# Differential attention whose scores contract all 128 rows against keys that are zero in the other component's rows

## The chip, the cores and the metric

The kernel runs on one core of one Trainium2 chip. The metric is the device time of one execution in microseconds (us); lower is better. Three executions of the kernel before took 3723.07, 3725.74 and 3731.34 us.

## The reference, cut to what matters

The model is a stack of five blocks on 512 tokens of width 1024: a first hybrid block, and then four layers with an mLSTM, a sliding-window attention, an HGRN2 and a differential attention as mixers, each followed by a feed-forward part. The change touches only the last mixer, the differential attention, with 8 heads of two components of 64 dimensions each:

```python
def diff_mixer(h, positions, lam_init, w_in, lam_vec, norm_w, w_out):
    ...
    q = partial_rope(proj[..., :w].reshape(bsz, seq, 2 * D_HEADS, D_HEAD_DIM), positions)
    k = partial_rope(proj[..., w:2 * w].reshape(bsz, seq, 2 * D_HEADS, D_HEAD_DIM), positions)
    ...
        s = jnp.einsum('bqhcd,bkhcd->bhcqk', qi, k, preferred_element_type=F32) * scale
        s = jnp.where(kpos[None, :] <= qpos[:, None], s, -jnp.inf)
        p = jax.nn.softmax(s, axis=-1)
        a = p[:, :, 0] - lam * p[:, :, 1]
        return jnp.einsum('bhqk,bkhe->bqhe', a, v)
```

Each component c of a head has its own 64 dimensions of queries and keys and its own softmax; the two weight matrices are subtracted and meet the same 128-wide values. Everything is float32.

## The kernel before, in words

Every engine runs a program written out by hand; they meet only through semaphores. `proj` holds the projections with features on the 128 partitions and tokens along the free dimension. In the differential layer, called part 3, tiles 0 to 7 of `proj` are the queries of heads 0 to 7 and tiles 8 to 15 are the keys. A head's component 0 lies in partitions 0 to 63 of its tile, and component 1 in partitions 64 to 127. The values lie in `df_v`.

The weights come as a stream of slots of 128x1024. For each slot SyncE issues a DMA, ScalarE makes the high part (line 1134), GpSimd subtracts it for the low part (`low`, line 532), and TensorE multiplies three times. The ring has four slots, so GpSimd is at most four slots ahead of TensorE: when the last value slot has been used, the last low part that can be made before the attention is that of the fourth slot of the output projection. The next needs a slot that the output projection frees, which comes after the attention.

VectorE copies the projected tiles out of PSUM and rotates them (`rope`, lines 1776 to 1778: a product with PSUM, a product of two SBUF tensors in place, and a sum of two SBUF tensors). In part 3 the query tiles are rotated before the first group of value tiles is copied out and the key tiles before the second. Then come the copies of the last values (line 1557), `lambdas` (lines 1941 to 1946, with one exponential on ScalarE), and one small copy (line 2040) that raises `mix_ready`, for which TensorE waits before its first score.

The attention is a pipeline over 64 jobs (`diff_jobs`): for each of 8 heads, for each of the 4 query blocks i of 128 tokens, for components 0 and 1. A job's score has (i+1)*128 keys. In step s TensorE issues the score of job s (line 802), the transposes of the weights of job s-2 (line 810, i+1 of them, full 128x128) and the products with the values of job s-3 (line 822, 128x128 each). VectorE adds the mask and takes the minimum (line 1626, from PSUM), and then scales the weights of the job before (line 1638 for component 0, line 1640 for component 1, from SBUF to SBUF). ScalarE makes the exponential (line 1224) and copies the transposed weights out of PSUM (line 1231). Before, a score is a matmul over the 64 rows of its component:

```python
jobs.append(job(proj[HD * c:HD * c + HD, hd, i * P:(i + 1) * P],
                proj[HD * c:HD * c + HD, 8 + hd, 0:w], w, lc[:, 768 - w:768],
```

A float32 matmul shows as two instructions in the trace, a transpose as one. The sliding-window layer and the dilated attention of the first block use the same `attention` function with full 128-row scores already, but with values of 64 columns. The stick-breaking code and the gated convolution of the first block (lines 580 to 587, on GpSimd) appear below only for their durations.

Of the kernel before, what the change touches and what calls it, by code (L numbers as in the profile page):

```python
# [8 lines left out]
F32 = mybir.dt.float32  # L9
# [3 lines left out]
ALU = mybir.AluOpType  # L13
# [3 lines left out]
P = 128  # L17
S = 512
D = 1024
DT = D // P  # L20
HD = 64
# [4 lines left out]
RING = 4  # L26
LEAD = 4
# [142 lines left out]
@contextmanager  # L170
def loop(eng, count):
    if count > 1:
        with eng.Fori(0, count) as i:
            yield i
    else:
        yield 0
# [16 lines left out]
def program(nc, xT, wstream, ada, cols, kept, bigc, layerc, pos, yT, parts):  # L193
    slots_total = stream_length(parts)
    ctx = ExitStack()
    with ctx:
# [82 lines left out]
        hg_p = [place(f"hg_p{r}", [P, TT, 640], F32, big + (16 + 4 * r) * S) for r in range(2)]  # L279
        hg_gate_at = [hg_k[:, 0, :]] + [proj[:, 8 + g, :] for g in range(7)]  # L280
        df_v = place("df_v", [P, TT, D], F32, big + 16 * S)

        bank = [ctx.enter_context(nc.psum_tensor(f"bank{b}", [P, S], F32)) for b in range(8)]

# [11 lines left out]
        def col(name, j=0, n=1):  # L296
# [29 lines left out]
                 "rope_ang", "ml_gate", "ml_pre", "ml_log", "ml_rows", "ml_turn", "ml_w", "ml_floor",  # L326
                 "ml_floor_kept", "ml_spread", "ml_diag", "ml_exp", "ml_a", "ml_den", "ml_num", "ml_out", "ml_sig",
                 "hg_lb", "hg_lbe", "hg_sig", "hg_dec", "hg_log", "hg_diff", "hg_e", "hg_qk", "hg_mm", "hg_put",
                 "hg_pv", "hg_out", "hg_gate", "hg_zero", "gate_kept", "lam_in", "lam_exp", "stored", "act_chain", "dve_chain"]
        sm = namedtuple("Semaphores", names)(*[ctx.enter_context(nc.semaphore(name)) for name in names])  # L330
        raw_loaded = [ctx.enter_context(nc.semaphore(f"raw_loaded{r}")) for r in range(RING)]
        ada_loaded = [ctx.enter_context(nc.semaphore(f"ada_loaded{r}")) for r in range(ADA_RING)]
# [4 lines left out]

        def job(q, k, width, bias_ap, values, **more):
            return dict(q=q, k=k, w=width, bias=bias_ap, v=values, sink=None, vis=None, gate=None, first=True,
                        last=True, dv=HD, row=0, dest=None) | more  # L340

        def head_pairs(heads):

# [44 lines left out]
        def diff_jobs():  # L388
            jobs = []
            for hd in range(8):  # L390
                for i in range(TT):
                    w = (i + 1) * P
                    for c in range(2):
                        jobs.append(job(proj[HD * c:HD * c + HD, hd, i * P:(i + 1) * P],
                                        proj[HD * c:HD * c + HD, 8 + hd, 0:w], w, lc[:, 768 - w:768],
                                        [(df_v[:, j, hd * P:(hd + 1) * P], P) for j in range(i + 1)],
                                        gate=lam if c else None, first=c == 0, last=c == 1, dv=P,
                                        dest=proj[:, hd, i * P:(i + 1) * P]))
            return jobs


# [126 lines left out]
        @block.gpsimd  # L528
        def _(pool):
            def low(k, i=0, step=0):  # L530
                pool.wait_ge(sm.hi_done, k + 1 + step * i)
                nc.gpsimd.tensor_tensor(w_lo[k % RING][:, :, :], raw[k % RING][:, :, :],  # L532
                                        w_hi[k % RING][:, :, :].bitcast(F32), ALU.subtract).then_inc(sm.lo_done, 1)

            def low_to(end):

                k, count = n["slot"], end - n["slot"]
                with loop(pool, count // RING) as i:
                    for q in range(RING):
                        low(k + q, i, RING)  # L540
                for q in range(count // RING * RING, count):
                    low(k + q)
                n.add(slot=count)

            def hgrn():

                for r in range(3):
                    nc.gpsimd.memset(hg_q[r][:, :], 0.0)
                    op = nc.gpsimd.memset(hg_t[r][:, :], 0.0)
                op.then_inc(sm.hg_zero, 1)  # L550
                pool.wait_ge(sm.hg_zero, 1)
                for hd in range(8):
                    for at in range(9):
                        m, i, b = hd * 10 + at, hd * 9 + at, LV[at]
                        if at == 6 and hd:
                            low(n["slot"])
                            n.add(slot=1)
                        pool.wait_ge(sm.hg_e, i + 1)
                        wait(pool, sm.hg_mm, m - 2)
                        d = halves(hg_d[i % 3][:, :], b)  # L560
                        nc.gpsimd.tensor_tensor(halves(hg_q[m % 3][:, :], b)[1], halves(proj[:, hd, :], b)[1], d[1],
                                                ALU.mult)
                        nc.gpsimd.tensor_tensor(halves(hg_t[m % 3][:, :], b)[0], halves(hg_k[:, hd, :], b)[0], d[0],
                                                ALU.mult).then_inc(sm.hg_qk, 2 if at == 8 else 1)

            n = Counts()
            def gated_convolution():

                g = nc.gpsimd
                steps = 0  # L570

                def link(ins):

                    nonlocal steps
                    steps += 1
                    ins.then_inc(sm.conv_step, 1)
                    pool.wait_ge(sm.conv_step, steps)

                pool.wait_ge(sm.lin_free, len(IN_PROJ["first"][0]))
                for t in range(2):  # L580
                    u, y, w = proj[:, 13 + t, :], proj[:, 11 + t, :], [col("conv_w", 3 * t + i) for i in range(3)]
                    link(g.tensor_tensor(u, u, y, ALU.mult))
                    link(g.tensor_scalar(y, u, w[2], None, ALU.mult))
                    for lag in (1, 2):
                        link(g.tensor_scalar(conv_tmp[:, lag:S], u[:, 0:S - lag], w[2 - lag], None, ALU.mult))
                        link(g.tensor_tensor(y[:, lag:S], y[:, lag:S], conv_tmp[:, lag:S], ALU.add))
                    link(g.tensor_tensor(proj[:, 2 + t, :], y, proj[:, 2 + t, :], ALU.mult))

            first_slot = 0
            for at, part in enumerate(parts):  # L590
                tiles, values = IN_PROJ[part]
                if part == "first":
                    low_to(len(tiles) + len(values) + 8 + LEAD)
                    gated_convolution()
                if part in (1, 3):
                    low_to(first_slot + LEAD)
                    pool.wait_ge(sm.lin_free, lin_total(parts[:at]))
                    pool.dma_start(rope_i[:, :], pos).then_inc(sm.pos_loaded, 16)
                if part == 2:
                    low_to(first_slot + len(tiles) + len(values) + LEAD)  # L600
                    hgrn()
                first_slot += stream_length([part])
            low_to(slots_total)
# [3 lines left out]
        def _(pe):  # L607
# [188 lines left out]
            def attention(jobs, bufs):  # L796
                a, g = n["att"], n["att_g"]
                for step in range(len(jobs) + 3):
                    if step < len(jobs):
                        j, it = step, jobs[step]  # L800
                        wait(pe, sm.att_ready, a + j - 1)
                        mm(bank[j % 2][:, 0:it["w"]], it["q"], it["k"], start=True,  # L802
                           stop=True).then_inc(sm.att_scores, 1)
                    if 2 <= step <= len(jobs) + 1:
                        j, it = step - 2, jobs[step - 2]
                        pe.wait_ge(sm.att_normed, a + j + 1)
                        wait(pe, sm.att_copied, a + j - 1)
                        at = 0
                        for t, (_, keys) in enumerate(it["v"]):
                            op = turn(bank[2 + j % 2][0:keys, t * P:(t + 1) * P], bufs["p"][j % 2][:, at:at + keys],  # L810
                                      ident)
                            at += keys
                        op.then_inc(sm.att_turned, 1)
                    if step >= 3:
                        j, it = step - 3, jobs[step - 3]
                        pe.wait_ge(sm.att_copied, a + j + 1)
                        if it["first"]:
                            g += 1
                            wait(pe, sm.att_out, g - 4)
                        out = bank[4 + g % 4][it["row"]:it["row"] + it["dv"], 0:P]  # L820
                        for t, (v, keys) in enumerate(it["v"]):
                            op = mm(out, v, bufs["pt"][j % 2][0:keys, t * P:(t + 1) * P],  # L822
                                    start=it["first"] and t == 0, stop=it["last"] and t == len(it["v"]) - 1)
                        op.then_inc(sm.att_pv, 1)
                n.add(att=len(jobs), att_g=sum(it["last"] for it in jobs))
# [1347 lines left out]
```

## Time and profile before

| | |
|---|---|
| three executions | 3723.07, 3725.74, 3731.34 us (median 3725.74) |
| span of the profiled execution | 3727.0 us; of the three times only 3731.34 lies above it, 4.3 us more |
| PE busy | 3469.8 us (93%) |
| DVE busy | 1692.0 us (45%) |
| ACT busy | 1215.5 us (33%) |
| POOL busy | 1381.3 us (37%) |
| the attention of part 3, first score to last value product | from 3136.3 to 3255.3 us of the span |

PE is TensorE's matmul stream and PEld its weight loads, which can lie under a running matmul; DVE is VectorE, ACT ScalarE, POOL GpSimd. PEclk is the clock that TensorE was granted, 1.00 for 2.4 GHz and 0.50 for 1.2 GHz. Ends of matmuls are modelled, so times between starts are read, not durations. A matmul's recorded start is that of its weight load where the load was not done ahead.

### The profile page before, as it was taken

The numbers are of one execution on the slowest core, as the hardware profiler recorded it, in microseconds if no ns is written. First come the engines' busy times: TensorE is split into PE (matmuls) and PEld (weight loads), VectorE is DVE, ScalarE is ACT, GpSimd is POOL, SyncE is SP. The second block draws the span as 40 slices with busy tenths as digits, with TensorE's granted clock in tenths as the row PEclk, the third lists the DMA queues.
The fourth block names the chain that finished last, engine by engine and source line by source line (L and its number), as shares of the span: only waits on it lengthen the run. The fifth ranks groups of instructions, "written<-read, shape, count | busy, mean of one in ns | idle before, by whom it ended". The sixth has DMA issues, their size and how long they took to land.

```text
span 3727.0 us, 44127 instructions
## 1 busy us (share of the span) xinstructions
PE 3469.8 (93%) x15724; PEld 2676.3 (72%) x15724; DVE 1692.0 (45%) x2677; ACT 1215.5 (33%) x1900; POOL 1381.3 (37%) x671
## 2 busy tenths in 40 slices
PE   7997999999989999889999988889999898989998
PEld 6754578886656888656788867656888685658886
DVE  2244455502245551576555036865553336562212
ACT  3235433223233322344332233333322322533322
POOL 3430144443223444302344435853444341024442
PEclk9969999999999999899999999989999998989998
DMA  4300145532214554201455322002554231013331
GB/s 136 100 30 1 34 158 186 191 109 79 61 45 136 187 194 121 82 23 57 147 186 186 112 75 79 23 23 85 197 181 155 89 96 40 1 46 102 96 102 62
DMA packets 101528, 374.12 MB, mean 100 GB/s; under 512 B 11280, under 2 KB 11408, under 8 KB 101136
## 3 DMA queue, kind: packets, MB, share of 16 engines
q1 hardware_dynamic: 101232, 371.76, 31.2%
q8 instruction: 88, 1.44, 0.2%
q0 software_dynamic: 160, 0.52, 0.0%
q14 instruction: 48, 0.39, 0.0%
HBM read 370.15 MB, written 2.10 MB: 100 GB/s over the span
## 4 chain that ended last, share of the span: by engine, by line
PE 79%; DVE 7%; ACT 2%; issue 1%; DMA 0%; POOL 0%; DVEq 0%; ACTq 0%
PE bank L617 18%; PE bank L619 18%; PE bank L618 18%; PE bank L705 3%; PE bank L802 2%; PE bank L706 2%; PE bank L707 2%; PE bank L822 2%; PE bank L810 1%; PE bank L661 1%; PE bank L663 1%; PE bank L662 1%; DVE hg_d L1892 1%; PE bank L1040 1%; DVE hg_p L1907 1%
## 5 line engine op out<-in xcount | busy, mean ns | idle before, releaser
L532 POOL TENSOR_TENSOR w_lo<-raw,w_hi 128x1024 fp32r<-128x1024 f32 x501 | 1234.9, 2469 | 2270.3 <-ACT w_hi L1134 2270.2
L1134 ACT ACTIVATE w_hi<-raw 128x1024 fp32r<-128x1024 f32 x501 | 527.5, 1058 | 1410.2 <-PE bank L619 1190.0
L617 PE MATMUL bank<-h_hi,w_hi 128*128 128x512 f32 x2264 | 884.7, 391 | 0.0
L619 PE MATMUL bank<-h_hi,w_lo 128*128 128x512 f32 x2264 | 881.7, 389 | 0.0
L618 PE MATMUL bank<-h_lo,w_hi 128*128 128x512 f32 x2264 | 881.7, 389 | 0.0
L617 PEld LDWEIGHTS bank<-h_hi,w_hi 128*128 128x128 f32 x2264 | 425.5, 188 | 89.2 <-issue 1.7
L619 PEld LDWEIGHTS bank<-h_hi,w_lo 128*128 128x128 f32 x2264 | 425.4, 188 | 89.2
L618 PEld LDWEIGHTS bank<-h_lo,w_hi 128*128 128x128 f32 x2264 | 425.5, 188 | 87.6
L1957 DVE SCALAR_TENSOR_TENSOR ada_acc<-ada_raw,cond,ada_acc 128x1024 f32<-128x1024 f32 x168 | 261.3, 1555 | 234.9 <-DMA ada_raw<-ada 233.0
L617 PE MATMUL bank<-hid_hi,w_hi 128*128 128x512 f32 x880 | 343.0, 390 | 0.4 <-DVE hid_lo L1973 0.4
L619 PE MATMUL bank<-hid_hi,w_lo 128*128 128x512 f32 x880 | 342.4, 389 | 0.0
L618 PE MATMUL bank<-hid_lo,w_hi 128*128 128x512 f32 x880 | 342.4, 389 | 0.0
L1973 DVE TENSOR_TENSOR hid_lo<-layer_const,hid_hi 128x512 f32 (+1 forms) x110 | 224.2, 2038 | 108.1 <-ACT hid_hi L1368 108.1
L1570 DVE SCALAR_TENSOR_TENSOR x<-bank,mod,x 128x512 f32<-128x512 f32 x64 | 48.0, 750 | 466.7 <-PE bank L619 443.7
L617 PEld LDWEIGHTS bank<-hid_hi,w_hi 128*128 128x128 f32 x880 | 165.2, 188 | 34.9 <-DVE hid_lo L1973 0.8
L619 PEld LDWEIGHTS bank<-hid_hi,w_lo 128*128 128x128 f32 x880 | 165.2, 188 | 34.4
L618 PEld LDWEIGHTS bank<-hid_lo,w_hi 128*128 128x128 f32 x880 | 165.2, 188 | 34.2
L705 PE MATMUL bank<-h_hi,w_hi 128*128 128x512 f32 x360 | 157.3, 437 | 33.2 <-DVE h_lo L1474 33.2
L1363 ACT ACTIVATE layer_const<-bank 128x512 f32<-128x512 f32 x110 | 65.5, 596 | 335.5 <-PE bank L619 312.4
L1970 DVE TENSOR_TENSOR layer_const<-bank,layer_const 128x512 f32<-128x512 f32 x110 | 75.8, 689 | 209.1 <-PE bank L619 184.2
L706 PE MATMUL bank<-h_lo,w_hi 128*128 128x512 f32 x360 | 151.8, 422 | 0.0
L707 PE MATMUL bank<-h_hi,w_lo 128*128 128x512 f32 x360 | 150.9, 419 | 0.0
(322 smaller groups left out, 4277.5 us busy)
## 6 DMA issues: line engine op xcount, KB each, us to landing
raw<-weights SPq DMA_DIRECT2D x501, 512.0 KB, 3.6
ada_raw<-ada SPq DMA_DIRECT2D x192, 512.0 KB, 4.4
layer_const<-layer_const SPq DMA_DIRECT2D x5, 512.0 KB, 4.6
x<-x_t SPq DMA_DIRECT2D x1, 2048.0 KB, 8.2
y_t<-x SPq DMA_DIRECT2D x1, 2048.0 KB, 6.3
tables<-big_const SPq DMA_DIRECT2D x1, 768.0 KB, 7.2
cols<-columns SPq DMA_DIRECT2D x1, 573.5 KB, 9.1
rope_i<-positions POOLq DMA_DIRECT2D x2, 256.0 KB, 4.6
```

What stands on the lines that cost most here:

```text
L532: nc.gpsimd.tensor_tensor(w_lo[k % RING][:, :, :], raw[k % RING][:, :, :], w_hi[k % RING][:, :, :].bitcast(F32), ALU.subtract).then_inc(sm ...
L617: mm(out, w_hi[r][:, at, :], hi, start=first and at == 0, stop=False)
L618: mm(out, w_hi[r][:, at, :], lo, start=False, stop=False)
L619: op = mm(out, w_lo[r][:, at, :], hi, start=False, stop=last and at == len(pairs) - 1)
L705: mm(out, w_hi[r][:, c, :], h_hi[:, c, :], start=c == 0, stop=False)
L706: mm(out, w_hi[r][:, c, :], h_lo[:, c, :], start=False, stop=False)
L707: op = mm(out, w_lo[r][:, c, :], h_hi[:, c, :], start=False, stop=c == DT - 1)
L802: mm(bank[j % 2][:, 0:it["w"]], it["q"], it["k"], start=True, stop=True).then_inc(sm.att_scores, 1)
L1134: fn(w_hi[t % RING][:, :, :], raw[t % RING][:, :, :], ACT.Copy).then_inc(sm.hi_done, 1)
L1957: op = v.scalar_tensor_tensor(ada_acc[:, :], ada_raw[a % ADA_RING][:, :], cond[:, kc:kc + 1], ada_acc[:, :], ALU.mult, ALU.add)
L1970: v.tensor_tensor(sil[q % 2], bank[(mt + 2 * q + 1) % 4][:, :], sil[q % 2], ALU.mult).then_inc(sm.lin_free, 2)
L1973: v.tensor_tensor(hid_lo[:, q + 4 * i, :], sil[q % 2], hid_hi[:, q + 4 * i, :].bitcast(F32), ALU.subtract).then_inc(sm.part_lo, 1)
```

## The change

The score of both components becomes one matmul over all 128 partitions: the stationary operand is the whole query tile of the head, and the moving operand is a key tile with zeros in the 64 rows of the other component. GpSimd makes both key tiles from the rotated keys, after the low parts of the slots up to the fourth of the output projection: it writes component 1's keys to a new buffer `df_k` (rows 0 to 63 zero) and then zeroes rows 64 to 127 of the key tile in place. `block64` is 1/64 within a component's block and 0 outside, so the product with it and 64 keeps or zeroes a row. Each pair waits for the head's rotation, the second operation for the first, and the first score of each head waits for `df_keys`.

```diff
+        df_k = place("df_k", [P, 8, S], F32, big + 33 * S)
...
-                        jobs.append(job(proj[HD * c:HD * c + HD, hd, i * P:(i + 1) * P],
-                                        proj[HD * c:HD * c + HD, 8 + hd, 0:w], w, lc[:, 768 - w:768],
+                        keys = df_k[:, hd, 0:w] if c else proj[:, 8 + hd, 0:w]
+                        jobs.append(job(proj[:, hd, i * P:(i + 1) * P], keys, w, lc[:, 768 - w:768],
                                         [(df_v[:, j, hd * P:(hd + 1) * P], P) for j in range(i + 1)],
                                         gate=lam if c else None, first=c == 0, last=c == 1, dv=P,
-                                        dest=proj[:, hd, i * P:(i + 1) * P]))
+                                        dest=proj[:, hd, i * P:(i + 1) * P], keys=hd + 1 if i + c == 0 else 0))
...
-                with loop(pool, count // RING) as i:
-                    for q in range(RING):
-                        low(k + q, i, RING)
+                if count >= RING:
+                    with loop(pool, count // RING) as i:
+                        for q in range(RING):
+                            low(k + q, i, RING)
...
+                if part == 3:
+                    low_to(first_slot + len(tiles) + len(values) + LEAD)
+                    for hd in range(8):
+                        pool.wait_ge(sm.rope_out, len(SWA_TILES) + 8 + hd + 1)
+                        k = proj[:, 8 + hd, :]
+                        nc.gpsimd.tensor_scalar(df_k[:, hd, :], k, block64[:, HD:HD + 1], float(HD), ALU.mult,
+                                                ALU.mult).then_inc(sm.df_moved, 1)
+                        pool.wait_ge(sm.df_moved, hd + 1)
+                        nc.gpsimd.tensor_scalar(k, k, block64[:, 0:1], float(HD), ALU.mult,
+                                                ALU.mult).then_inc(sm.df_keys, 1)
...
                         wait(pe, sm.att_ready, a + j - 1)
+                        wait(pe, sm.df_keys, it["keys"])
```

## Rows read from the trace of the kernel before

**Rows 1.** The page, engine totals: busy us, share of the span, instructions.

```profile
PE 3469.8 (93%) x15724; PEld 2676.3 (72%) x15724; DVE 1692.0 (45%) x2677; ACT 1215.5 (33%) x1900; POOL 1381.3 (37%) x671
```

**Rows 2.** Stretches: start:end, length, PE, PEld, DVE, ACT, POOL busy, PEclk, DMA.

```profile
3140.00:3160.00 20.00, 20.00 (x70) 12.66 (x70) 8.05 (x34) 7.19 (x22) 0.00 (x0) 0.59 0.00 0
...
3180.00:3200.00 20.00, 20.00 (x119) 14.07 (x117) 12.93 (x54) 12.02 (x35) 0.00 (x0) 1.00 0.00 1
```

**Rows 3.** Chain in order of time: start, length, what; two value products of 512.

```profile
3158.06 0.89 PE bank L822 x8
...
3240.37 0.89 PE bank L822 x8
```

**Rows 4.** Timeline, steady attention of part 3: start, length, engine, line, operation.

```profile
3164.85 1.12 PE L802 MATMUL bank<-proj 64*128 64x512 f32 x2
...
3165.91 0.31 PEld L810 LDWEIGHTS bank<-kept,att_p_late 128*128 128x128 f32 x3 [0.76 <-DVE att_p_late L1640]
...
3166.29 0.61 PE L822 MATMUL bank<-att_pt_late,df_v 128*128 128x128 f32 x4
...
3166.83 1.12 PE L802 MATMUL bank<-proj 64*128 64x512 f32 x2
```

**Rows 5.** Timeline, dilated attention of the first block, scores over 128 rows.

```profile
381.01 1.13 PE L802 MATMUL bank<-key_rows,proj 128*128 128x512 f32 x2
...
381.55 0.14 PEld L810 LDWEIGHTS bank<-kept,att_p_first 128*128 128x128 f32 x1 [0.24 <-DVE att_p_first L1640]
381.98 0.49 PE L810 MATMUL bank<-kept,att_p_first 128*128 128x128 f32 x3
...
394.67 1.13 PE L802 MATMUL bank<-key_rows,proj 128*128 128x512 f32 x2
```

**Rows 6.** Timeline, mLSTM: a 4-row matmul, then 128-row matmuls only.

```profile
986.65 1.12 PE L967 MATMUL bank<-ml_rows,layer_const 4*128 4x512 f32 x2
987.70 2.42 PE L969 MATMUL bank<-proj 128*128 128x512 f32 x8
989.96 2.32 PE L982 MATMUL bank<-ml_a,kept 128*128 128x512 f32 x8
992.12 4.04 PE L986 MATMUL bank<-ml_a,ml_v 128*128 128x512 f32 x13
```

**Rows 7.** Timeline, the same steady attention: what releases the transposes of a 512-wide job.

```profile
3167.99 0.69 DVE L1626 CUSTOM_DVE_ANT_0 att_s_late<-bank,layer_const 128x512 f32<-128x512 f32 x1 [0.69 <-PE bank L802]
...
3168.80 0.48 DVE L1640 TENSOR_SCALAR att_p_late<-att_p_late,small 128x512 f32<-128x512 f32 x1
...
3169.45 0.66 PE L810 MATMUL bank<-kept,att_p_late 128*128 128x128 f32 x4
```

**Rows 8.** Timeline and stretches: first scores and the clock, sliding window, then part 3.

```profile
1620.63 2.50 PE L802 MATMUL bank<-swa_k,proj 128*128 128x128 f32 x6 [7.46 <-DVE swa_k L2032]
...
1630.00:1635.00 5.00, 5.00 (x30) 3.37 (x28) 4.20 (x22) 3.11 (x10) 0.00 (x0) 0.94 0.01 2
...
3136.29 0.80 PE L802 MATMUL bank<-proj 64*128 64x128 f32 x4 [10.45 <-DVE small L2040]
...
3154.44 0.79 PE L802 MATMUL bank<-proj 64*128 64x128 f32 x2
...
3156.00:3158.00 2.00, 2.00 (x15) 1.76 (x14) 0.69 (x5) 0.98 (x3) 0.00 (x0) 0.91 0.00 0
```

**Rows 9.** Timeline, the end of the input projection of part 3.

```profile
3125.28 2.34 POOL L532 TENSOR_TENSOR w_lo<-raw,w_hi 128x1024 fp32r<-128x1024 f32 x1 [4.81 <-ACT w_hi L1134]
3125.62 2.55 DVE L1777 TENSOR_TENSOR proj<-proj,rope_cs 128x512 f32<-128x512 f32 x1
...
3129.42 0.68 DVE L1777 TENSOR_TENSOR proj<-proj,rope_cs 128x512 f32<-128x512 f32 x1
```

**Rows 10.** Timeline, first block: GpSimd's tensor_scalar beside VectorE's attention.

```profile
225.15 1.57 POOL L585 TENSOR_SCALAR conv_tmp<-proj,cols 128x511 f32<-128x511 f32 x1
...
225.88 0.25 DVE L1636 SCALAR_TENSOR_TENSOR att_p_first<-att_p_first,small,layer_const 128x31 f32<-128x31 f32 x1
```

More of the change, by code:

```diff
@@ L328, in program @@
                  "hg_lb", "hg_lbe", "hg_sig", "hg_dec", "hg_log", "hg_diff", "hg_e", "hg_qk", "hg_mm", "hg_put",
-                 "hg_pv", "hg_out", "hg_gate", "hg_zero", "gate_kept", "lam_in", "lam_exp", "stored", "act_chain", "dve_chain"]
+                 "hg_pv", "hg_out", "hg_gate", "hg_zero", "gate_kept", "df_moved", "df_keys", "lam_in", "lam_exp", "stored", "act_chain", "dve_chain"]
         sm = namedtuple("Semaphores", names)(*[ctx.enter_context(nc.semaphore(name)) for name in names])
@@ L339, in job @@
             return dict(q=q, k=k, w=width, bias=bias_ap, v=values, sink=None, vis=None, gate=None, first=True,
-                        last=True, dv=HD, row=0, dest=None) | more
+                        last=True, dv=HD, row=0, dest=None, keys=0) | more
         def head_pairs(heads):
```

## The prediction

> **What bounds the kernel now.** I read the page's engine totals first: TensorE is busy 93% of the span [rows 1], so something pays only if it shortens TensorE's stream or one of the stretches in which it waits. The change touches one stage, the attention of part 3. The table of stretches comes next [rows 2]: from 3180 to 3200 us TensorE is busy all 20 us at full clock while VectorE has 12.9 and ScalarE 12.0, so TensorE's own order of work sets the pace; from 3140 to 3160 its granted clock is 0.59, that is, 1.2 GHz for most of it. GpSimd does nothing there. The chain in order of time gives the period of a head: six heads lie between the value products at 3158.06 and 3240.37, so 13.72 us each [rows 3]. Last comes the timeline, for what that period is made of.
>
> **What a change of shape costs TensorE.** In the mLSTM four 128-row float32 products of 512, 384, 256 and 128 columns (1280 in all, line 982) take 992.12 - 989.96 = 2.16 us from start to start [rows 6], 0.216 us per 128 columns, with no gap. A head has 20 blocks of scores and 20 of value products at 0.216 and 20 transposes at half of that (one instruction): 4.32 + 4.32 + 2.16 = 10.8 us. The period is 13.72, so 2.92 us per head, 0.365 per job, are something else. The timeline shows where [rows 4]. A 512-wide score should take 0.864 and takes 3165.91 - 3164.85 = 1.06, so 0.20 too much. Two value blocks should take 0.43 and take 0.54, 0.11 too much. Three transposes take 0.38 for 0.324, 0.055 too much. Together 0.365. The weight load of the transposes begins only when the score has ended, at 3165.91 [rows 4]. In the dilated attention, whose score has 128 rows, that load begins at 381.55, under the running score, and the same score takes 381.98 - 381.01 = 0.97 [rows 5]. And in the mLSTM the step from a 4-row to a 128-row product costs 987.70 - 986.65 - 0.864 = 0.19 us before it and 989.96 - 987.70 - 2.16 = 0.10 at its start, while the next, 128 rows to 128 rows, costs nothing [rows 6]. So a weight load isn't done ahead across a change of the tile's shape, and each job of the differential attention has two such changes: value product (128 rows) to score (64), and score to transpose (128).
>
> The Trainium skill has the rule, in "TensorEngine Tiling (Array Packing)", Tiling Modes, Key Properties: changing the tiling mode drains TensorE. The trace agrees, with 0.10 us of drain and 0.10 of uncovered load at a change. The Trainium skill also has, in "TensorE: Matmul & The Clock Gate", Why this matters for your kernels, that a single matmul over 32 rows takes as long as one over 128; by that alone the change moves nothing on TensorE, a rival below.
>
> **The change part by part.**
>
> *Scores over 128 rows, heads 1 to 7.* Same columns, no change of shape any more: the 0.20 and the 0.11 of each job go, the 0.055 at the transposes I leave. TensorE alone would then need 10.8 + 8*0.055 = 11.24 us per head. What is late next is VectorE's chain. From the start of the second 512-wide score at 3166.83 the mask and minimum start at 3167.99, the scaling of the job before at 3168.80, ending at 3169.28, and the transposes start 0.17 later, at 3169.45: 2.62 us [rows 4, 7], 2.52 once the score's weight load is done ahead. TensorE's path between the same two points shrinks to 0.864 (score) + 0.38 (three transposes) + 0.65 (six value instructions) + 0.216 (score) = 2.11, so it waits 0.4 there. By the same count the 256-wide jobs, where the score to come is short against that chain, wait some 0.2. Hence 11.24 + 0.6 = 11.8 us per head, 1.9 less than 13.72, and 7 heads give 13.4 us. Bounds: from above a head can't be under 11.24 (17.4 us gained); from below only the 0.09 us of rows 5 against rows 4 may go, 0.72 per head, 5.0 us gained. I take 11.8, because both changes of shape are priced in rows 6.
>
> *The clock at the start.* In the sliding-window attention, with 128-row scores, the first score starts at 1620.63 and the granted clock is at 0.94 in the stretch from 1630: about 10 us at 1.2 GHz. In part 3 the first score starts at 3136.29 and the clock is up only within 3156 to 3158, some 20 us [rows 8], though TensorE is busy nearly all the time from 3140. The scores over half of the rows are the difference I see. Head 0 takes 3154.44 - 3136.29 = 18.15 us, all of it at the lower clock. Without changes of shape it would be near 16 (an estimate: the excess of 0.31 per job of rows 4, for the eight jobs, is 2.5, and the first jobs wait for VectorE anyway), and with the clock back after 10 us the remaining 6 take 3: 13 us. The 1.7 us at the start of head 1 that still ran at half clock return another 0.9.
>
> *GpSimd's key tiles.* 16 tensor_scalar operations of 128x512. One of that kind took 1.57 us [rows 10], with the semaphore between two about 1.65, so 26 us. They start when the last low part is done, at 3125.28 + 2.34 = 3127.6 [rows 9]. By then six of the eight key tiles are rotated, and the last product of the rotation starts at 3129.42 [rows 9], so the pair of head 0 is ready before 3132, ahead of the first score at 3136.3, and head h's pair by 3128 + 3.3*(h+1), far ahead of a head per 12 us. So the new wait `df_keys` holds nothing back; its eight waits are worth 0.1 us each at most if one keeps a load from being done ahead. Nothing is queued behind the operations on GpSimd: the next low part needs a slot that is free only after the attention. SyncE's queue isn't touched, and the split of GpSimd's loop falls into its idle time.
>
> *What they do to VectorE.* This is the price. While GpSimd makes a low part from 3125.28 to 3127.62, the rotation's in-place product, which takes 0.68 alone, takes 2.55 and ends 0.55 after GpSimd [rows 9]. So an operation of VectorE on two SBUF tensors waits for GpSimd's to end. In the changed kernel GpSimd is busy from 3127.6 without a break, and VectorE's work in just that stretch is what the first score waits for: line 1778 of tile 14, 1777 and 1778 of tile 15, and line 1941. One after another with an operation of GpSimd between them, they end about 1.35, 2.25, 3.6 and 4.3 us later; the copies of `df_v` come from PSUM and take what they took. So the first score starts 4.3 us later, near 3140.6. Bounds: nothing, if a tensor_scalar with one input doesn't block (a small operation on two SBUF tensors took its ordinary 0.25 at 225.88, in the middle of one [rows 10]), and 6.5 if the small ones of `lambdas` wait too. I take 4.3: the large operations are the ones like the row that was blocked. After that some ten operations of GpSimd remain, and in head 0 VectorE's scalings wait 0 to 1.57 us each; with the lower clock most of it is hidden, so I add 2 us, and head 0 takes 15 instead of 18.15 (bounds 12.6 and 19.2, so 5.5 gained to 1 lost).
>
> The Trainium skill, "SBUF — State Buffer", on the shared port pair, says that GpSimd and a VectorE operation with two SBUF inputs exclude each other for the whole instruction. Rows 9 agree (ended 0.55 us after GpSimd), the small operation of rows 10 doesn't; by the skill's rule the start would come 4.3 to 6.5 us later, by rows 10 not at all.
>
> **The sum.** -13.4 (heads 1 to 7) - 0.9 (clock in head 1) - 3.1 (head 0) + 4.3 (start) = -13.1 us. The profiled execution's span of 3727.0 would become 3713.9. The span lies 1.3 us above the median of the three times, so I take the difference off the median: 3712.6 us.
>
> **The rivals.**
>
> *Half of the gain.* The load is done ahead only from score to transpose, and the other 0.1 us turns up elsewhere. For it: the dilated attention has 128-row scores and yet a period of 394.67 - 381.01 = 13.66 us [rows 5], no better than 13.72. Against it: its values have 64 columns, so it has two changes of shape too, at other places. It gives -5.0 - 0.9 - 1.5 + 4.3 = -3.1, 3722.6 us.
>
> *Nothing on TensorE.* Rows of the array don't matter, as dilated attention's period suggests: 8 heads gain 13.72 - 13.66 each, 0.5 us; the clock gives the same 0.9 and 1.5, the start costs 4.3: +1.4, 3727.1 us. Against it stand rows 6.
>
> *All of it.* GpSimd's one-input operations don't block and VectorE's chain has more slack than I count: -17.4 - 0.9 - 5.5 = -23.8, 3701.9 us. For it rows 10; against it rows 7 and 9.
>
> *Slower, by the shared port.* The period of a head stays 13.66 as in rows 5 (0.06*8 = 0.5 us gained), the start comes 6.5 us later, and in head 0 each of the eight scalings waits a full 1.57, 12.6 us in all: +18.6, 3744.3 us. It decides from the point at which GpSimd's 26 us cost VectorE more than the gain on TensorE; at my gain of 17.4 that needs nearly every operation to be waited for in full. Against it is that TensorE's steps in head 0 are long at the lower clock, and rows 6 price the gain.
>
> **How the numbers follow.** Chances: the forecast 0.68, half of the gain 0.15, nothing on TensorE 0.04, all of it 0.08, slower 0.05. The time is that of the forecast, 3712.6. Its own range is 3706 to 3719; the range of 3703 to 3723 takes in half of the gain and nearly all of the best case, and leaves out the slower one and some of either side. A difference of over 0.2%, 7.5 us, is about what can be told here: the forecast but for 0.04 of it and the best case are faster, 0.72; that 0.04, half of the gain and nothing on TensorE are no difference, 0.23; slower 0.05.
>
> **What the changed kernel's profile would show.** The weight load of the transposes (line 810) starting under the score, and a 512-wide score to its transposes in 0.87 us; the chain of line 822 with a period of 11.8 us per head and idle spells before line 810 released by lines 1638 and 1640; the granted clock at 1.00 about 10 us after the first score; lines 1777, 1778 and 1941 ending with GpSimd's operations and the first score near 3140.6. I am wrong if the period stays above 13, if VectorE isn't delayed before the first score, or if the clock still takes 20 us to rise.

## The result and the profile after

| | before | changed |
|---|---|---|
| executions beside the first measurement (median) | 3723.07 to 3731.34 us (3724.62) | 3697.61 to 3709.60 us (3705.38) |
| ratio of the times, 95% interval | | 0.9939 (0.9923 to 0.9954) |
| profiled execution: span, time | 3727.0 us | 3707.8 us, 3709.6 us |
| attention of part 3: first score to first square sum of the norms | 120.1 us | 98.3 us |

The change makes the kernel faster by 0.6%: 0.0061 of 3725.74 is 22.7 us, with an interval from 17.1 to 28.7. The forecast was 13.1 us. A second measurement of the changed kernel, on another occasion, gave 0.9940 (0.9927 to 0.9954).

The page of the changed kernel, engine totals, which answer to [rows 1]:

```profile
PE 3450.2 (93%) x15724; PEld 2671.0 (72%) x15724; DVE 1701.2 (46%) x2677; ACT 1217.3 (33%) x1900; POOL 1392.1 (38%) x687
```

TensorE has as many instructions as before and 19.6 us less of busy time, GpSimd 16 instructions and 10.8 us more. The chain in order of time of the changed kernel (start, length, what), answering to [rows 3]; line 835 is line 822 of before:

```profile
3155.00 0.89 PE bank L835 x8
...
3225.25 0.89 PE bank L835 x8
```

Six heads in 70.25 us, 11.71 us each, where it was 13.72. The timeline of the changed kernel in the same place of a head as [rows 4, 7] (line 815 is 802, line 823 is 810, line 1639 is 1626, line 1653 is 1640):

```profile
3159.24 1.02 PE L815 MATMUL bank<-proj 128*128 128x512 f32 x2
...
3159.82 0.53 PEld L823 LDWEIGHTS bank<-kept,att_p_late 128*128 128x128 f32 x3 [0.39 <-DVE att_p_late L1653]
3160.10 0.49 PE L823 MATMUL bank<-kept,att_p_late 128*128 128x128 f32 x3
...
3160.43 0.61 PE L835 MATMUL bank<-att_pt_late,df_v 128*128 128x128 f32 x4
3160.76 0.30 PEld L815 LDWEIGHTS bank<-df_k,proj 128*128 128x128 f32 x2
3160.87 1.02 PE L815 MATMUL bank<-df_k,proj 128*128 128x512 f32 x2
...
3162.73 0.39 PE L815 MATMUL bank<-proj 128*128 128x128 f32 x2
...
3163.29 0.55 PE L823 MATMUL bank<-kept,att_p_late 128*128 128x128 f32 x3 [0.17 <-DVE att_p_late L1653]
```

The weight load of the transposes (3159.82) lies under the score, and that of the next score (3160.76) under the value products. The 512-wide score takes 0.86 us to the next instruction instead of 1.06, two value blocks 0.44 instead of 0.54, three transposes 0.33 instead of 0.38. At 3163.29 TensorE waits for VectorE: the 128-wide score before it should take 0.22 and takes 0.56.

The start of the stage, stretches of the changed kernel (columns as in [rows 2]) and the timeline ahead of them, answering to [rows 8] and [rows 9] (lines 1789 to 1791 are 1776 to 1778 of before, 606 and 609 are the new operations):

```profile
3140.00:3145.00 5.00, 4.95 (x14) 3.33 (x15) 2.99 (x14) 2.54 (x10) 3.46 (x6) 0.50 0.00 0
3145.00:3150.00 5.00, 4.91 (x24) 2.78 (x24) 3.57 (x13) 3.15 (x9) 0.00 (x0) 0.95 0.00 0
```

```profile
3128.16 2.34 POOL L533 TENSOR_TENSOR w_lo<-raw,w_hi 128x1024 fp32r<-128x1024 f32 x1 [4.81 <-ACT w_hi L1147]
...
3130.48 1.13 POOL L606 TENSOR_SCALAR df_k<-proj,kept 128x512 f32<-128x512 f32 x1
3131.08 1.06 DVE L1791 TENSOR_TENSOR proj<-proj,rope_t 128x512 f32<-128x512 f32 x1
3131.70 1.00 POOL L609 TENSOR_SCALAR proj<-proj,kept 128x512 f32<-128x512 f32 x1
...
3132.67 0.68 DVE L1790 TENSOR_TENSOR proj<-proj,rope_cs 128x512 f32<-128x512 f32 x1
3132.68 1.22 POOL L606 TENSOR_SCALAR df_k<-proj,kept 128x512 f32<-128x512 f32 x1
3133.38 1.06 DVE L1791 TENSOR_TENSOR proj<-proj,rope_t 128x512 f32<-128x512 f32 x1
...
3134.97 0.69 POOL L606 TENSOR_SCALAR df_k<-proj,kept 128x512 f32<-128x512 f32 x1
...
3136.86 0.38 DVE L1954 TENSOR_TENSOR small<-cols 128x128 f32<-128x128 f32 x1
...
3139.95 0.77 PE L815 MATMUL bank<-proj 128*128 128x128 f32 x2 [11.24 <-POOL proj L609]
```

From the start of the last low part to the first score it is 11.79 us, and was 11.01: a delay of 0.8. It is all in three operations of VectorE: the two sums of line 1791 take 1.06 each and took 0.69, and the first small one of `lambdas`, line 1954, takes 0.38 and took 0.29. Each sum ends some 0.5 us after the operation of GpSimd that it started in, as the product of [rows 9] did. The releaser named at 3139.95 is a GpSimd operation, but the pair of head 0 had ended at 3132.70; the last thing to come was VectorE's small copy, as before. The clock is back after about 3145.5 (a tenth of the stretch at half), 5.5 us after the first score, where it took 20. Head 0 lasts from 3139.95 to 3151.0, 11.1 us, and lasted 18.15.

The stage adds up: head 0 -7.1, heads 1 to 7 from 96.9 (7*13.72, and 0.87 for the clock) to 7*11.71 = 82.0, -14.9, the tail +0.2: -21.8; with the start's +0.8 it is -21.0. The two single spans differ by 19.2 only, because the changed kernel's was 2.9 us late when it came to the stage and took 1.0 us less after it (469.6 instead of 470.6), both in parts that the change doesn't touch. Over the traces below the first score lies anywhere from 3123 to 3140 us, so a single span can't settle this, and lengths within the stage can: the period from head 2 on repeats to 0.02 us.

### The profile page after: what moved, and what is told of

It is laid out like the page before. It is cut to its first block, busy times and chain, and to the rows that moved or that the text cites. A ratio compares the mean times of both kernels' runs of the same rounds, so it can differ in the third digit from the quotient of the medians.

```text
span 3707.8 us, 44151 instructions
## 1 busy us (share of the span) xinstructions
PE 3450.2 (93%) x15724; PEld 2671.0 (72%) x15724; DVE 1701.2 (46%) x2677; ACT 1217.3 (33%) x1900; POOL 1392.1 (38%) x687
## 4 chain that ended last, share of the span: by engine, by line
PE 75%; DVE 6%; issue 5%; ACT 2%; POOL 2%; DMA 0%; DVEq 0%; POOLq 0%; ACTq 0%
PE bank L629 18%; PE bank L630 18%; PE bank L631 18%; PE bank L717 2%; PE bank L718 2%; PE bank L719 2%; PE bank L815 2%; PE bank L835 2%; POOL w_lo L533 1%; DVE hg_d L1905 1%; PE bank L1053 1%; PE bank L823 1%; DVE hg_p L1920 1%; PE bank L673 1%; PE bank L674 1%
## 5 line engine op out<-in xcount | busy, mean ns | idle before, releaser
L631 PE MATMUL bank<-h_hi,w_lo 128*128 128x512 f32 x2264 | 881.6, 389 | 0.0
L1970 DVE SCALAR_TENSOR_TENSOR ada_acc<-ada_raw,cond,ada_acc 128x1024 f32<-128x1024 f32 x168 | 274.2, 1632 | 234.7 <-DMA ada_raw<-ada 233.3
L1561 DVE COPY proj<-bank 128x512 f32<-128x512 f32 x68 | 46.3, 690 | 229.8 <-PE bank L631 211.6
```

Of the source, the lines that this page charges most:

```text
L631: op = mm(out, w_lo[r][:, at, :], hi, start=False, stop=last and at == len(pairs) - 1)
L1970: op = v.scalar_tensor_tensor(ada_acc[:, :], ada_raw[a % ADA_RING][:, :], cond[:, kc:kc + 1], ada_acc[:, :], ALU.mult, ALU.add)
```

## Experiments

All of them are the changed kernel with one edit. "Period" is the time between the first scores of two neighbouring heads from head 2 on (head 1 can begin at the lower clock, or beside GpSimd), "head 0" is from the stage's first score to head 1's. Where a run has one time only, the medians of the kernel before beside it are 3726.8 us (head0_half, head0_rows), 3727.4 (extra64, extra128, one_op) and 3725.8 (two_input). Times of one kernel differ by 10 us and more from execution to execution, so nothing below rests on a single time; the lengths of the stages are read from the traces.

| run | head 0 | period | last low part to first score | ratio to before (95%), or one time |
|---|---|---|---|---|
| before | 18.15 | 13.72 | 11.0 | |
| changed | 11.07 | 11.71 | 11.8 | 0.9939 (0.9923 to 0.9954) |
| pool_only | 18.31 | 13.72 | 11.8 | 1.0008 (0.9996 to 1.0020) |
| rows_only | 10.48 | 11.71 | 11.0 | 0.9953 (0.9936 to 0.9969) |
| head0_half | 18.16 | 11.70 | | 3718.0 us |
| head0_rows | 11.18 | 13.72 | | 3716.0 us |
| extra64 | 14.86 | 14.71 | | 3729.7 us |
| extra128 | 13.57 | 12.82 | | 3705.9 us |
| one_op | 11.26 | 11.70 | 11.7 | 3704.3 us |
| two_input | 11.28 | 11.71 | 13.1 | 3715.0 us |

**Where the gain comes from: the two halves of the change.** pool_only keeps GpSimd's work and goes back to 64 rows:

```diff
-                        keys = df_k[:, hd, 0:w] if c else proj[:, 8 + hd, 0:w]
-                        jobs.append(job(proj[:, hd, i * P:(i + 1) * P], keys, w, lc[:, 768 - w:768],
+                        src = df_k[:, hd, 0:w] if c else proj[:, 8 + hd, 0:w]
+                        rows = slice(HD * c, HD * c + HD) if True else slice(0, P)
+                        keys = src[rows, :]
+                        jobs.append(job(proj[rows, hd, i * P:(i + 1) * P], keys, w, lc[:, 768 - w:768],
```

> GpSimd makes the key tiles as in the changed kernel, but each score contracts only the 64 rows of its component (component 0 from the key tile, component 1 from df_k), as before. Theory (the gain is TensorE's, from the changes of tile shape that are gone): the period of a head stays 13.7 us, the clock rises some 20 us after the first score, the first score comes 0.8 us later than before counted from the last low part; no gain, 0 to +2 us against the kernel before. Rival (part of the gain comes from another layout of the keys or from GpSimd's loop): more than 3 us faster than before.

The chain of pool_only in order of time has the old period:

```profile
3173.49 0.89 PE bank L837 x8
...
3187.22 0.89 PE bank L837 x8
```

The ratio is 1.0008 (0.9996 to 1.0020), so GpSimd's work alone costs at most 0.2% and gives nothing; the start has the changed kernel's 11.8 us. rows_only does the other half, the edit `keys = proj[:, 8 + hd, 0:w]` for both components and no operations on GpSimd (it leaves out the zeros, so its scores are not the model's):

> Scores over all 128 rows, but GpSimd makes no key tiles: both components read the unmasked key tile (the zeros are left out, so the two components' scores are sums of both). Theory: the whole gain of the changed kernel and the start's 0.8 us: period 11.7 us per head, head 0 about 11, 20 to 24 us faster than before. Rival (GpSimd's contention in head 0 costs the changed kernel several us more): 26 us or more.

The period is 11.71 and the stage takes 97.7 us, as expected, but the start is back at 11.0, without the 0.8: that is GpSimd's. Head 0 is 0.6 us shorter than in the changed kernel, and most of that is the clock's: it comes back 4.5 us after the first score (3130.07) and not 5.5.

```profile
3130.00:3135.00 5.00, 4.93 (x15) 3.22 (x16) 2.76 (x14) 2.46 (x10) 0.00 (x0) 0.55 0.00 0
```

One us less at half clock is worth 0.5 of the 0.6, so GpSimd's contention in head 0 costs some 0.1 us by this estimate, not "several us". The ratio is 0.9953 (0.9936 to 0.9969), 12 to 24 us; its middle, 17.5, lies below the 20 to 24 expected, and the interval takes in both the expectation's lower part and the changed kernel's own ratio. The times don't tell the two apart.

**What head 0 gains, and why.** The same slice as in pool_only, but only for head 0 (head0_half), or for all heads but head 0 (head0_rows):

> The changed kernel with the scores of head 0 alone over 64 rows. Theory (the clock's early return in head 0 comes from what TensorE does there): head 0 takes 16 to 18.5 us instead of 11.1, the clock comes back 15 to 20 us after the first score, heads 1 to 7 keep 11.7 us. Rival (the early return is chance, the phase of the clock's changes against the stage): head 0 takes 11 to 14 us.

> The scores of head 0 alone over 128 rows, of heads 1 to 7 over 64. Theory: head 0 takes about 11 us and the clock is back within 5 to 9 us of the first score; heads 1 to 7 have a period of 13.7 us; some 6 us faster than before. Rival (chance of phase): head 0 stays at 15 to 18 us.

Stretches of head0_half, then of head0_rows, columns as above:

```profile
3150.00:3155.00 5.00, 5.00 (x13) 2.66 (x12) 1.61 (x6) 1.85 (x6) 0.00 (x0) 0.50 0.00 0
3155.00:3160.00 5.00, 5.00 (x23) 3.88 (x22) 2.38 (x9) 1.63 (x4) 0.00 (x0) 0.57 0.00 0
```

```profile
3132.00:3137.00 5.00, 4.58 (x13) 3.19 (x14) 3.08 (x15) 2.30 (x9) 3.88 (x6) 0.50 0.00 0
3137.00:3142.00 5.00, 5.00 (x24) 3.04 (x23) 3.32 (x14) 2.85 (x10) 0.00 (x0) 0.89 0.00 0
```

With the first score at 3139.94, head0_half has its clock back at about 3159.3 (a share of 0.86 of the stretch at half gives 0.57), 19.4 us after. head0_rows starts at 3132.37 and is back at 3138.1, 5.7 us after. Head 0 takes 18.16 and 11.18 us, the other heads keep the period of their own kind. The theory holds on both sides. The other traces speak against phase too: with 64-row scores in head 0 the clock comes back 19.4 to 21.0 us after the first score (before, pool_only, head0_half), with 128-row scores and no extra matmul 4.5 to 6.0 us after (eight traces, one_op, two_input and the widened version of below among them), wherever the first score lies. So here the clock stays at 1.2 GHz for some 14 us longer with 64-row scores, though PE is shown busy in nearly all of that time.

**Is it the change of shape, or are 64 rows slow in themselves?** A small float32 matmul ahead of the transposes of each job, into the bank that they overwrite, over 64 rows (extra64) or over 128 (extra128):

```diff
                         at = 0
+                        if bufs is AT["late"] and it["dv"] == P:
+                            mm(bank[2 + j % 2][:, 0:8], ident[0:HD, :], ones[0:HD, 0:8], start=True, stop=True)
                         for t, (_, keys) in enumerate(it["v"]):
```

> The changed kernel with one small matmul more per job ahead of the transposes, over 64 rows and 8 columns, into the bank that the transposes then overwrite: the 128-row stream is broken by two changes of shape per job, with almost no work. Theory (the change of shape costs, not the rows): 0.3 to 0.4 us per job more, less what hid in waits for VectorE: period 13.5 to 14.5 us, nearly all of the gain of heads 1 to 7 given back. Rival (scores over 64 rows are slow in themselves): 0.05 to 0.1 us per job more, period 12.0 to 12.5.

> The control: the same small matmul over 128 rows and 8 columns, no change of shape. Theory and rival alike: period 11.8 to 12.6 us; the difference to the 64-row one is the price of two changes of shape per job, 0.2 to 0.35 us by the theory, nothing by the rival.

The timeline of extra64, then of extra128, both at a 256-wide score; line 823 is the small matmul, 825 the transpose:

```profile
3182.15 0.60 PE L815 MATMUL bank<-proj 128*128 128x256 f32 x2
3182.67 0.29 PEld L823 LDWEIGHTS bank<-kept 64*128 64x128 f32 x2 [0.33 <-issue]
3182.67 0.39 PE L823 MATMUL bank<-kept 64*128 64x8 f32 x2
...
3182.99 0.33 PE L825 MATMUL bank<-kept,att_p_late 128*128 128x128 f32 x1
```

```profile
3181.32 0.60 PE L815 MATMUL bank<-proj 128*128 128x256 f32 x2
3181.55 0.41 PEld L823 LDWEIGHTS bank<-kept 128*128 128x128 f32 x2
3181.76 0.28 PE L823 MATMUL bank<-kept 128*128 128x8 f32 x2
...
3181.90 0.31 PE L825 MATMUL bank<-kept,att_p_late 128*128 128x128 f32 x1
```

Over 64 rows the load begins when the score has ended (3182.67), and the score's step is 0.52 and the small matmul's 0.32. Over 128 rows the load lies under the score, and the steps are 0.44 and 0.14: two changes of shape cost 0.26 us here. The periods are 14.71 and 12.82, 1.89 us per head or 0.24 per job, inside the 0.2 to 0.35 of the theory. Both expected ranges for the period itself were too low (13.5 to 14.5, 11.8 to 12.6): even over 128 rows the extra matmul costs 0.14 us per job, with its own two weight loads. The loss appears though all scores have 128 rows, so it is the change of shape that costs, and no 64-row score is needed for it. What a stream of 64-row matmuls alone would do no run shows.

The two also bear on the clock: both have it back 9 us after the first score (stretches of extra64 from 3139 at 0.59, of extra128 from 3131 at 0.61, first scores at 3134.07 and 3125.79). So the changes of shape made no difference to the clock, and what holds it down in head0_half is that its scores have 64 rows, not the changes of shape that come with them. Why both take 9 rather than 5.5 us stays open.

```profile
3139.00:3144.00 5.00, 5.00 (x17) 3.12 (x18) 1.79 (x6) 1.74 (x6) 0.00 (x0) 0.59 0.00 0
```

```profile
3131.00:3136.00 5.00, 5.00 (x20) 3.55 (x20) 2.30 (x9) 2.03 (x7) 0.00 (x0) 0.61 0.00 0
```

**Why the start cost 0.8 us and not 4.3.** The operations took 0.69 us alone and not 1.57, and VectorE was held for 0.8 us in all. In the changed kernel both readings fit, that VectorE waits for the end of an operation that is merely short, and that it isn't held for the whole. one_op takes the second multiplication away, so that the form is the convolution's:

```diff
-                        nc.gpsimd.tensor_scalar(df_k[:, hd, :], k, block64[:, HD:HD + 1], float(HD), ALU.mult,
-                                                ALU.mult).then_inc(sm.df_moved, 1)
+                        nc.gpsimd.tensor_scalar(df_k[:, hd, :], k, block64[:, HD:HD + 1], None,
+                                                ALU.mult).then_inc(sm.df_moved, 1)
```

> GpSimd's two tensor_scalar operations per head with one multiplication instead of two (the factor 64 is left out, so the keys are 64 times too small). Theory (the form with one operation is the slow one, 1.57 us as in the convolution, and what I mis-sized was the form): each takes about 1.57 us, VectorE's rotation waits longer, the first score comes 3 to 5 us after where it stood before, counted from the last low part, as forecast for operations of that length, and head 0 takes 12 to 15 us. Rival (0.69 is the time of a product with a column of this kind whatever the number of operations, the convolution's was slow for another reason): 0.69 us each, start and head 0 as in the changed kernel.

The timeline of one_op:

```profile
3127.04 2.12 POOL L609 TENSOR_SCALAR proj<-proj,kept 128x512 f32<-128x512 f32 x1
3127.13 0.67 DVE L1790 TENSOR_TENSOR proj<-proj,rope_cs 128x512 f32<-128x512 f32 x1
3127.84 0.98 DVE L1791 TENSOR_TENSOR proj<-proj,rope_t 128x512 f32<-128x512 f32 x1
...
3129.14 1.57 POOL L606 TENSOR_SCALAR df_k<-proj,kept 128x512 f32<-128x512 f32 x1
...
3130.79 1.56 POOL L609 TENSOR_SCALAR proj<-proj,kept 128x512 f32<-128x512 f32 x1
```

The first half of the theory holds: one multiplication takes 1.57 us and two take 0.69. The second half falls: with GpSimd's operations that long the first score still comes 11.7 us after the last low part's start. Within GpSimd's operation of 3127.04 VectorE's product takes its ordinary 0.67 (it starts 0.09 after it, and the recorded times of GpSimd are rough), and the sum at 3127.84, well inside, takes 0.98 instead of 0.69 and ends 0.34 before GpSimd's does. GpSimd's own operation grows, from 1.57 to 2.12. So mere length isn't what costs: here VectorE did not wait for the end of GpSimd's tensor_scalar. Head 0 isn't longer either: 11.26 us, where 12 to 15 was expected, although GpSimd is at work through all of it. two_input asks whether the kind of operation decides, with `tensor_tensor(df_k[:, hd, :], k, block64[:, HD:HD + 1].to_broadcast([P, S]), ALU.mult)` and the like for the key tile:

> GpSimd makes the key tiles with tensor_tensor operations of two inputs (the key tile and one column of the mask, broadcast; the factor 64 is left out). Theory (it is the kind of GpSimd's operation that decides whether VectorE's two-input operations are held: tensor_tensor holds them for its whole length as the low parts do, tensor_scalar doesn't): each takes some 1.26 us, lines 1790 and 1791 end with GpSimd's operations, and the first score comes 14 to 16 us after the last low part's start instead of 11.8. Rival (what holds VectorE is the size of the low parts, or GpSimd yields between its operations anyway): 11.5 to 12.5 us.

```profile
3130.20 1.37 POOL L609 TENSOR_TENSOR proj<-proj,kept 128x512 f32<-128x512 f32 x1
...
3131.53 1.48 POOL L606 TENSOR_TENSOR df_k<-proj,kept 128x512 f32<-128x512 f32 x1
3132.15 1.41 DVE L1791 TENSOR_TENSOR proj<-proj,rope_t 128x512 f32<-128x512 f32 x1
3133.09 1.37 POOL L609 TENSOR_TENSOR proj<-proj,kept 128x512 f32<-128x512 f32 x1
...
3134.42 1.04 POOL L606 TENSOR_TENSOR df_k<-proj,kept 128x512 f32<-128x512 f32 x1
```

An operation of GpSimd takes 1.04 alone and up to 1.49 beside VectorE, VectorE's sum 1.41 instead of 0.69, and the first score comes 13.1 us after the last low part's start, 1.3 later than in the changed kernel. That lies between the two expectations. Two inputs do hold VectorE longer than one: the sum at 3132.15 ends at 3133.56, 0.55 after GpSimd's operation, exactly as in [rows 9]. At 1.04 us a piece there is less to wait for than I had put in. What all these rows have in common: beside GpSimd's two-input operations VectorE's two-input ones are late by up to the operation's length, beside its one-input ones by 0 to 0.4 us, whether these last 0.69 or 1.57. Why the two kinds differ stays open.

**A version that is faster by its stages.** If changes of shape cost, the 64-column value products of the dilated and of the sliding-window attention should be widened too. Both heads' values lie side by side, so the product takes all 128 columns and the copy takes the 64 rows that belong to the head:

```diff
-                                [(swa_v[:, j, kv * HD:(kv + 1) * HD], P) for j in range(lo, i + 1)],
-                                sink=neg_sinks[:, hd:hd + 1], row=b, dest=q))
+                                [(swa_v[:, j, :], P) for j in range(lo, i + 1)], dv=P,
+                                take=slice(HD * kv, HD * kv + HD), sink=neg_sinks[:, hd:hd + 1], dest=q))
...
-                        rows = slice(it["row"], it["row"] + it["dv"])
+                        rows = it["take"] or slice(it["row"], it["row"] + it["dv"])
```

> The changed kernel, and also the value products of the dilated (16 jobs) and of the sliding-window attention (64 jobs) over 128 columns of values instead of 64, so that they have no change of shape either; the copy takes the 64 rows that belong to the head. Theory: dilated attention's cycle of 8 jobs falls from 13.66 to about 11.7 us (4 us in all); in the sliding-window attention TensorE would save up to 0.3 us per job but VectorE, busy 87% there, becomes the bound at some 1.25 us per job instead of 1.43: about 8 us; together 8 to 14 us less than the changed kernel, 27 to 36 less than before. Rival (only a change of rows costs, not of columns): nothing more than the changed kernel's gain, about -19 to -23.

It was run twice, the second time beside the changed kernel:

> The changed kernel with 128 columns of values in the dilated and the sliding-window attention, beside the changed kernel. Theory: in the first run its sliding-window and dilated stages were shorter by the trace, and the group norms after the differential attention happened to run 5 us longer at the lower clock; 8 to 12 us less than the changed kernel. Rival (the longer spell at the lower clock belongs to the version): 2 to 5 us less.

> The changed kernel once more, on the chip on which its widened version runs. Theory: its attention stage is 21.8 us shorter in the trace, so the ratio to the kernel before lies near 0.994 (-20 to -24 us). Rival (the stage's gain is partly given back later): 0.996 or more.

The ratios to before are 0.9919 (0.9900 to 0.9938) and 0.9931 (0.9917 to 0.9944) for the widened version, 0.9940 (0.9927 to 0.9954) for the changed kernel beside the second. The first is 30 us less than before (23 to 37), inside the 27 to 36 expected. The timeline of wide_both in the dilated attention, answering to [rows 5]:

```profile
382.47 1.02 PE L815 MATMUL bank<-key_rows,proj 128*128 128x512 f32 x2
383.33 0.49 PE L823 MATMUL bank<-kept,att_p_first 128*128 128x128 f32 x3
...
394.37 1.02 PE L815 MATMUL bank<-key_rows,proj 128*128 128x512 f32 x2
```

A cycle of eight jobs takes 11.90 us and took 13.66. In the sliding-window attention the instructions of the score's line, with first and last start, are these, in the changed kernel's second run and in wide_again:

```profile
L815 PE MATMUL bank<-swa_k,proj x128: 275/379/796, 1620.4 to 1710.0; 128*128 128x256 f32 x96, 128*128 128x128 f32 x32
```

```profile
L815 PE MATMUL bank<-swa_k,proj x128: 275/379/793, 1614.5 to 1696.9; 128*128 128x256 f32 x96, 128*128 128x128 f32 x32
```

89.6 us became 82.4. Columns cost like rows, so the rival is out for the stages. Of the whole time the version took 5.4 us less than the changed kernel beside it by the medians (3699.32 against 3704.73), 3.4 by the ratios, with intervals that overlap: below the 8 to 12 expected, and not told apart from nothing. That it is faster is shown for its stages, not for the whole. The expectation's remark on the group norms is half settled: what follows the attention took 475.3 us instead of 469.6 to 470.8 in three of the traces, wide_both's, but also changed_again's and two_input's, so it doesn't belong to the version.

## Why the prediction was too small

The direction and the mechanism on TensorE were right. Two terms failed: how long head 0 stays at the lower clock and waits for GpSimd, and how long GpSimd's operations hold VectorE at the start. By its own terms:

- *Scores over 128 rows, heads 1 to 7: -13.4 forecast, -14.1 measured.* The period was to be 11.8 and is 11.71. The prices of rows 4 to 6 were right, extra64 against extra128 shows them as the cause, and so was what is late next: from the second 512-wide score to the transposes it is 2.42 us (2.52 forecast), TensorE idle for 0.34 (0.4 forecast). One thing was left out: the 0.055 at the transposes was part of the change of shape too and went (0.33 for three).
- *Clock in head 1: -0.9*, as forecast.
- *Head 0: -3.1 forecast, -7.1 measured.* This is the larger mis-sized term. The clock came back 5.5 us after the first score, not 10 as I took over from the sliding-window attention [rows 8]: 4.5 us less at half clock, worth some 2.2 us. Contention with GpSimd cost some 0.1 us (rows_only against the changed kernel, the clock taken off), not 2, and hardly more in one_op, whose operations last 1.57. The 16 us for a head without changes of shape at the lower clock were about right: 16.6, an estimate, twice what 11.07 less half of 5.5 leaves. head0_half and head0_rows show that the cause I named, 64-row scores, was the right one.
- *Start: +4.3 forecast, +0.8 measured.* The step that failed is that an operation of VectorE on two SBUF tensors waits for GpSimd's to end: I took it from [rows 9], where GpSimd's operation has two inputs, and applied it to one-input operations. The 1.57 us was also the price of another form, but one_op has operations of that length and its start is no later. The row that spoke against the step, in [rows 10], was in the forecast as a bound and was the nearer one: it was the only row of that kind of operation. The Trainium skill's rule on the shared port pair ("SBUF — State Buffer", Terms) says that the loser is blocked for the whole instruction. It fits the low parts and two_input here, but not tensor_scalar in one_op, where VectorE's sum began and ended inside one of GpSimd's operations.
- *df_keys holds nothing back*: right, head 0's pair was ready 7.3 us ahead.

Of the four, two were off in the same direction, by 4.0 and 3.5 us. The start lay inside its bounds, head 0 1.6 us beyond its better one (5.5), since that bound still went by a clock that needs 10 us. So the result, 3703.0 us by the ratio (3697.0 to 3708.6), came out at the very end of the range of 3703 to 3723, and half of its interval lies beyond; the range was drawn as if both would hardly go well together.

The rivals: by the number the best case, *all of it* (3701.9 us), was nearer than the forecast. Half of the gain and nothing on TensorE are excluded by the period; the slower case by pool_only, in which all of GpSimd's work costs 0.0008 of the time (-0.0004 to 0.0020). *All of it* had the right side for two of its terms, the start and head 0, and the wrong one for the third: VectorE's chain had no more slack than counted.

## What to carry to other kernels

In a stream of short 128-row matmuls on TensorE a 64-row one was dearer than a zero-padded full one: look in the timeline for a weight load that starts only when the matmul before it has ended, and count the changes of shape per job, rows and columns alike. This stage, which starts at the lower clock, stayed there longer with scores over half of the rows, so padding paid twice at its start; it may in another. Price an operation on a shared resource from a row of the very same kind, and not from a larger one of another kind. And before a difference of half a us is put down to contention, look when the clock came back.

## What the runs showed of the hardware that was not expected

- GpSimd's tensor_scalar of 128x512 float32 with a column and a constant (two multiplications) takes 0.69 us, with the column alone 1.57.
- VectorE's two-input sum began and ended inside one of GpSimd's tensor_scalar operations and took 0.98 us instead of 0.69 (3127.84 in one_op); GpSimd's operation took 2.12 instead of 1.57. Beside a GpSimd operation with two inputs the same sum took 1.41 and ended 0.55 after it (two_input).
- With the same TensorE instructions but for the rows of head 0's scores, the granted clock went from 1.2 to 2.4 GHz 19.4 (head0_half, 64 rows) or 5.5 us (the changed kernel, 128 rows) after the first score.
